# Order of the first modulation groups, shifts of half the channels added as a bias of the input projection, and the first scale group in two halves of 256 columns

## The reference, cut to what matters

```python
mods_x = jnp.split(silu_c @ w_mod[l] + b_mod[l], N_MOD, axis=-1)    # six vectors of 2048
mods_c = jnp.split(silu_cc @ w_mod[l] + b_mod[l], N_MOD, axis=-1)
nc = modulated_norm(h_c, attn_norm[l], mods_c[0], mods_c[1])        # rmsnorm(h) * (1 + scale) + shift
pc = nc @ w_in[l][:, Q_END:KR_END]                                  # 256 + 64 columns
nx = modulated_norm(h_x, attn_norm[l], sa_x, sca_x)
q_a, kv_a, k_rope, g_b, g_c, hh = jnp.split(nx @ w_in[l], [...], axis=-1)   # 512, 256, 64, 3 x 1024 columns
```

## Time and profile before

| | us |
|---|---|
| median of three runs | 1111.26 (1111.02 to 1112.99) |
| span of the profiled execution | 1107.5 |
| between the two | 3.8 |
| PE busy | 1011.4 (91%) |
| VectorE busy | 549.5 (50%) |
| ScalarE busy | 221.2 (20%) |
| GpSimd busy | 20.3 (2%) |
| DMA, mean over the span | 343 GB/s, 380.3 MB |

### The profile page before, as it was taken

One profiled execution on the slowest core, in us unless ns is written; L12 is line 12 of the kernel. 1 busy time (PEld: TensorE's weight loads), 2 busy tenths in 40 slices (PEclk: granted clock), 3 DMA queues, 4 the chain that ended last, 5 costly groups with the idle time before them and its releaser, 6 DMA issues.

```text
span 1107.5 us, 15664 instructions
## 1 busy us (share of the span) xinstructions
PE 1011.4 (91%) x6004; PEld 566.6 (51%) x6005; DVE 549.5 (50%) x1082; ACT 221.2 (20%) x442; POOL 20.3 (2%) x28
## 2 busy tenths in 40 slices
PE   3889999999999889999998999998899898998985
PEld 2534578888885345444485645433334333344421
DVE  3000186854824694985582234545246344545524
ACT  5211110000002363010341213222113112213212
POOL 0000000000002001000000000000000000000002
PEclk9899999999999999999999999999999998999998
DMA  9999979999854747999739999999999999999994
GB/s 358 389 389 389 377 232 359 372 345 328 284 181 169 256 144 262 387 387 335 230 130 367 371 405 403 406 408 407 409 409 406 408 407 408 409 407 408 409 406 180
DMA packets 158359, 380.30 MB, mean 343 GB/s; under 512 B 10498, under 2 KB 44112, under 8 KB 157136
## 3 DMA queue, kind: packets, MB, share of 16 engines
q1 hardware_dynamic: 158288, 379.35, 91.3%
HBM read 377.22 MB, written 2.10 MB: 342 GB/s over the span
## 4 chain that ended last, share of the span: by engine, by line
PE 64%; DMA 13%; SPq 12%; DVE 6%; issue 2%; ACT 2%; POOL 0%; ACTq 0%; DVEq 0%; POOLq 0%
PE ps L654 64%; DMA ring<-in_w_exp_down 7%; SPq L537 4%; SPq L532 4%; DVE part L1590 3%; DMA ring<-in_w_exp_up 2%; DMA ring<-in_w_in 1%; DMA ring<-in_w_mod 1%; DMA qnT<-in_w_mod 1%; SPq L397 1%; DVE tiny L1736 1%; SPq L417 1%; DVE xres L2021 1%; SPq L394 1%; SPq L395 0%
## 5 line engine op out<-in xcount | busy, mean ns | idle before, releaser
L654 PE MATMUL ps<-nreg,ring 128*128 128x256 f32 (+2 forms) x1312 | 306.9, 398 | 6.7 <-DVE ring L1741 4.1
L654 PEld LDWEIGHTS ps<-nreg,ring 128*128 128x128 f32 (+1 forms) x1312 | 243.8, 190 | 63.1 <-issue 30.8
L1590 DVE SCALAR_TENSOR_TENSOR part<-ring,csT,part 128x512 f32<-128x512 f32 x232 | 174.7, 753 | 8.6
L654 PE MATMUL ps<-ring,nreg 128*32 128x512 f32 (+1 forms) x1344 | 174.2, 602 | 3.6 <-DMA ring<-in_w_exp_up 3.2
L654 PE MATMUL ps<-ring,conv 128*32 128x512 f32 (+2 forms) x688 | 104.5, 663 | 23.0 <-DMA ring<-in_w_exp_down 22.1
L654 PE MATMUL ps<-ring 128*128 128x512 f32 x256 | 110.7, 592 | 0.0
L654 PEld LDWEIGHTS ps<-ring,nreg 128*32 128x32 f32 (+1 forms) x1344 | 49.1, 115 | 111.7 <-issue 111.6
L2021 DVE TENSOR_TENSOR xres<-xres,ps 128x512 f32<-128x512 f32 x96 | 61.6, 683 | 48.9 <-PE ps L654 48.9
L654 PEld LDWEIGHTS ps<-ring 128*128 128x128 f32 x256 | 48.6, 190 | 60.4 <-issue 60.0
L654 PEld LDWEIGHTS ps<-ring,conv 128*32 128x32 f32 (+2 forms) x688 | 30.2, 125 | 88.4 <-issue 83.9
L654 PE MATMUL ps<-pick,qnT 128*128 128x128 bf16 x384 | 67.8, 221 | 2.8 <-DMA ring<-in_w_exp_up 2.8
(11 more groups left out here) (265 smaller groups left out, 883.9 us busy)
## 6 DMA issues: line engine op xcount, KB each, us to landing
ring<-in_w_mod SPq DMA_DIRECT2D x78, 1024.0 KB, 10.9
ring<-in_w_exp_gate SPq DMA_DIRECT2D x128, 512.0 KB, 13.6
ring<-in_w_exp_up SPq DMA_DIRECT2D x128, 512.0 KB, 15.1
ring<-in_w_exp_down SPq DMA_DIRECT2D x128, 512.0 KB, 14.4
ring<-in_w_in SPq DMA_DIRECT2D x12, 2048.0 KB, 13.4
ring<-in_w_out SPq DMA_DIRECT2D x8, 2048.0 KB, 11.6
ring<-in_w_mod SPq DMA_DIRECT2D x3, 2048.0 KB, 19.7
ring<-in_w_in SPq DMA_DIRECT2D x3, 1664.0 KB, 15.7
```

Of the source, the lines that this page charges most:

```text
L654: return nc.tensor.matmul(o, l, r, start=start, stop=stop)
L1590: ins = V.scalar_tensor_tensor(out=out_, in0=w_, scalar=scale, in1=acc_, op0=ALU.mult, op1=ALU.add)
```

## The change

It does six things.

1. The groups come in the order scale 0, scale 1, scale 2, shift 2, scale 3, shift 3, shift 0, shift 1 (`MOD_ORDER`). Sets 0 and 1 are projected with scaled, unshifted tokens; sets 2 and 3 as before.
2. For sets 0 and 1 (`LATE = 2`) the product of the shift with the input weights is made by itself (`shift_products`), turned into columns (`bias_columns`) and added as a bias where ScalarE and VectorE read the projection's results. The latent tokens of these sets get their shift added by VectorE behind their last query use, for the convolution (`nT_shift`).
3. The first scale group is loaded as two halves of 256 columns (each half over all 16 row blocks, rows of 1 KB), with the first input-weight slice between and behind them, and worked in halves (`half_rows`, `half_cols`, `first_scale`).
4. Each group's row transposes move behind a projection block. The latent transposes start before the small columns.
5. The first convolution iteration is written out by itself. Its first block runs in two parts around the shift products; the statistics and the key rotation (`in_squares`) run in it, behind the first block of the second slice. GpSimd adds the squares of the channel blocks, so PE sums one product each. On VectorE the bias and the gains stand between the accumulations of groups 8 and 9.
6. The second convolution slice waits for `shift_full` 2 where it waited for `q_full` 1. Some semaphores are merged, with the counts that belong to them.

The core of the diff, SyncE first, then PE:

```diff
-        MOD_ORDER = [g for s in range(4) for g in (s, s + 4)]
+        MOD_ORDER = [4, 5, 6, 2, 7, 3, 0, 1]
+        LATE = 2
...
-            for s in range(2):
-                sp.dma_start(k_of(s, 8), mod_block(MOD_ORDER[0], 8 * s, 8)).then_inc(w_full[s], 16)
+            for h in range(2):
+                at = MOD_ORDER[0] * 512 + 256 * h
+                sp.dma_start(k_of(h, KC), wm[:, :, at:at + 256]).then_inc(w_full[h], 16)
+                for ks in (slice(2, 4),) if h else (slice(0, 1), slice(1, 2)):
+                    load_in(0, ks)
...
-            for s in range(1, 4):
-                for n in (2 * s, 2 * s + 1):
-                    load_early(n)
-                if s == 1:
-                    sp.wait_ge(mod_rows, 1)
-                load_in(s)
+            sp.wait_ge(mod_rows, 1)
+            load_in(1, slice(0, 4))
+            load_early(2)
+            load_in(2, slice(0, 4))
+            load_early(3)
+            load_early(4)
+            load_in(3, slice(0, 4))
+            for n in (5, 6, 7):
+                load_early(n)
...
             load_group(8, 12, mslot, freed_by_pe)
-            sp.wait_ge(q_full, 1)
+            sp.wait_ge(shift_full, 2)
             load_conv(0, 1, CONV0 + 2 * CW)
...
+            query_set(0, (0, 2), (0, 1))
+            pe.wait_ge(xT_ctx, KC // 2)
+            query_set(0, (1, 3), (0, 1))
+            pe.wait_ge(first_dve, 2)
+            half_rows(1)
+            rotary_set(0, (0, 1))
+            kv_set(0, 0, (0, 1))
+            half_cols(1)
+            kv_set(0, 1, (0, 1))
+            query_set(0, range(4), (2, 3))
+            pe.wait_ge(modT_done, 1)
+            second_rows()
+            rotary_set(0, (2, 3))
+            kv_set(0, 0, (2, 3))
+            mod_cols_of(1, 1, 7)
+            kv_set(0, 1, (2, 3))
+            for s in range(1, SETS):
+                query_set(s, range(4))
+                step_group(2 * s)
+                kv_set(s, 0)
+                mod_cols_of(2 * s, 0, 7)
+                step_group(2 * s + 1)
                 rotary_set(s)
+                mod_cols_of(2 * s + 1, 1, 7)
                 kv_set(s, 1)
...
+            def shift_products():
+                pe.wait_ge(shift_ready, LATE)
+                pe.wait_ge(q_sq, 4)
+                for bank, at, end in ((2, 0, QL), (3, QL, WI)):
+                    for k in range(4 * LATE):
+                        ins = mm(ps[32 * (k % 4):32 * (k % 4) + 32, bank, 0:end - at], shift_cols[:, k, :],
+                                 wiq[k // 4][:, k % 4, at:end], k < 4, k >= 4 * LATE - 4)
+                    ins.then_inc(shift_full, 1)
...
+            def in_squares():
+                pe.wait_ge(sq_added, 2)
+                mm(ps[:, 7, 0:T], ones, q_squ[:, 0:T], True, True).then_inc(stat_full, 1)
+                pe.wait_ge(kr_sum, 1)
+                mm(ps[:, 6, :], cst[:, C_DUP:C_DUP + P], krs[:, :], True, True)
+                mm(ps[:, 7, T:2 * T], cst[:, C_ROTK:C_ROTK + P], krs[:, 0:T], True, True).then_inc(kr_mm, 1)
+                pe.wait_ge(kv_out, 1)
+                pe.wait_ge(sq_added, 3)
+                mm(ps[:, 4, :], ones, squ[:, 1024:1536], True, True).then_inc(stat_full, 1)
...
-            with pe.Fori(0, 4) as i:
+            pe.wait_ge(w_full[0], 16 * 3)
+            pe.wait_ge(q_sq, 2)
+            first_conv(range(4 * LATE, KC))
+            shift_products()
+            first_conv(range(4 * LATE))
+            bias_columns()
+            conv_blocks(0, 0, BANKS_C, (1,))
+            conv_blocks(0, 1, BANKS_H, (0,))
+            in_squares()
+            conv_blocks(0, 1, BANKS_H, (1,))
+            pe.wait_ge(kv_out, 2)
+            mod_sum_cols(8, 0)
+            pe.wait_ge(gc_out, 2)
+            pe.wait_ge(mean_wide, 2)
+            conv_blocks(0, 2, BANKS_B)
+            mod_sum_cols(9, 1)
+            with pe.Fori(1, 4) as i:
```

And VectorE, from the last shifts to the loop:

```diff
+            accumulate(8, 0, by_feature=True)
+            ve.wait_ge(shift_full, 3)
+            V.tensor_copy(tiny[:, 16:28], ps[:, 7, 384:396])
+            V.tensor_copy(tiny[0:64, 28:30], ps[0:64, 7, 396:398]).then_inc(shift_ready, 1)
...
             kv_gain(0)
-            ve.wait_ge(stat_q, 1)
+            kv_gain(1)
+            ve.wait_ge(stat_full, 1)
+            ve.wait_ge(kr_mm, 1)
+            ve.wait_ge(q_out, 4)
             mean_square_wide(rowq, ps[:, 7, 0:T], QL)
...
+            accumulate(9, 1, by_feature=True)
+            conv_rows(0)
+            conv_products(0)
+            with ve.Fori(1, 4) as i:
+                accumulate(2 * i + 8, 0, by_feature=True)
+                accumulate(2 * i + 9, 1, by_feature=True)
+                conv_rows(i)
+                conv_products(i)
```

More of the change, by code:

```diff
@@ L1267, in _ @@
                     .then_inc(xT_ctx, 1)
[L1268 to L1269 removed]
             sc.wait_ge(xT_ctx, KC // 2)
[L1271 to L1278 removed]
+            for s, ks in ((0, (0, 1)), (0, (2, 3)), (1, range(4, 8)), (2, range(8, 12)), (3, range(12, 16))):
+                if s == 0 and ks[0] == 2:
+                    sc.wait_ge(mod_rows, 1)
+                    copy(part[:, 0, 256:512], ps[:, 7, 256:512]).then_inc(part_full, 1)
+                for n in ((), (1,), (2, 3), (4, 5))[s]:
+                    rows_out(n, 7, n % 2, n == 1)
+                sc.wait_ge(amul_ready, s + 1 + (ks[0] > 0))
+                for k in ks:
+                    if s < LATE:
+                        ins = nc.scalar.activation(nT[:, k, T:2 * T], nT[:, k, T:2 * T], ACT.Identity, scale=amul[:, k, 1:2])
+                    else:
+                        ins = nc.scalar.activation(nT[:, k, T:2 * T], nT[:, k, T:2 * T], ACT.Identity, bias=modT[:, k, 1:2],
+                                                   scale=amul[:, k, 1:2])
+                    ins.then_inc(nT_ctx, 1)
@@ L1281, in _ @@
             for m in range(4):
                 sc.wait_ge(q_full, m + 1)
-                nc.scalar.activation(squ[:, T * m:T * m + T], ps[:, m, 0:T], ACT.Square).then_inc(q_sq, 1)
+                copy(q_raw[:, m, :], ps[:, m, 0:T]).then_inc(q_sq, 1)
+            for n in (6, 7):
+                rows_out(n, 7, n % 2, False)
+            for n in range(2):
+                sc.wait_ge(shift_full, n + 1)
+                at, end, bank = ((0, QL, 2), (QL, WI, 3))[n]
+                copy(shift_rows[:, at:end], ps[:, bank, 0:end - at]).then_inc(shift_out, 1)
@@ L1284, in _ @@
+            sc.wait_ge(shift_ready, LATE + 1)
+            for m in range(4):
+                sc.wait_ge(q_sq, m + 1)
+                nc.scalar.activation(q_squ[:, T * m:T * m + T], q_raw[:, m, :], ACT.Square, bias=in_bias[:, m, 0:1])\
+                    .then_inc(q_sq, 1)
             sc.wait_ge(kr_full, 1)
-            copy(krs[:, :], ps[:, 6, :]).then_inc(kr_sum, 1)
+            for v in range(2):
+                ins = nc.scalar.activation(krs[:, T * v:T * v + T], ps[:, 6, T * v:T * v + T], ACT.Identity,
+                                           bias=in_bias[:, 6, v:v + 1])
@@ L1612, in _ @@
+            latent_out(range(4))
+            small_out()
+            latent_out((4, 5))
             ve.wait_ge(squares, 4)
-            rsqrt(tiny[:, 10:12], stat[:, 2:4], D)
+            V.tensor_scalar(tiny[:, 10:12], stat[:, 2:4], 1.0 / D, EPS, ALU.mult, ALU.add).then_inc(mean_sq, 1)
+            roots[0] += 1
+            latent_out((6, 7))
+            ve.wait_ge(root, roots[0])
             V.tensor_scalar(ctxs[:, 0, :], ctxs[:, 0, :], tiny[:, 10:11], None, ALU.mult).then_inc(ctxs_ready, 1)
-            cols_out(0, MOD_ORDER[0], 7)
@@ new lines, in _, with scale_of @@
+            first_scale(0)
+            first_scale(1)
+            def scale_of(n):
+                cols_out(n, MOD_ORDER[n], 7)
+                ve.wait_ge(modT_done, n + 1)
+                at = 4 * MOD_ORDER[n]
+                link(V.tensor_tensor(modT[:, at:at + 4, :], modT[:, at:at + 4, :],
+                                     bT[:, at:at + 4].unsqueeze(2).to_broadcast([P, 4, 2]), ALU.add))
+                return V.scalar_tensor_tensor(out=amul[:, at - 16:at - 12, :], in0=modT[:, at:at + 4, :], scalar=1.0,
+                                              in1=vecT[:, V_AN + at - 16:V_AN + at - 12].unsqueeze(2).to_broadcast([P, 4, 2]),
+                                              op0=ALU.add, op1=ALU.mult)
@@ new lines, in shift_of @@
+            def shift_of(n, out_):
+                cols_out(n, MOD_ORDER[n], 7)
+                ve.wait_ge(modT_done, n + 1)
+                at = 4 * MOD_ORDER[n]
+                return V.tensor_tensor(out_, modT[:, at:at + 4, :], bT[:, at:at + 4].unsqueeze(2).to_broadcast([P, 4, 2]), ALU.add)
+            for s in range(1, SETS):
+                n = (0, 1, 2, 4)[s]
+                if s < LATE:
+                    scale_of(n).then_inc(amul_ready, 1)
+                else:
+                    link(scale_of(n))
+                    shift_of(n + 1, modT[:, 4 * s:4 * s + 4, :]).then_inc(amul_ready, 1)
+                ve.wait_ge(amul_ready, s + 2)
```

(15 more changed lines are left out.)

310 lines of the change are left out of this document (153 added, 157 removed).

## The result

| | before | changed |
|---|---|---|
| median | 1110.84 us (1107.23 to 1112.99, 20 runs) | 1111.97 us (1108.31 to 1114.62, 20 runs) |
| ratio, 95% interval | | 1.0018 (1.0010 to 1.0026) |
| span of the profiled execution | 1107.5 | 1109.8 |
| second iteration starts | 189.53 | 189.42 |
| projection behind the convolution starts | 319.28 | 321.07 |

By the ratio the changed kernel is slower by 2.0 us (the two medians lie 1.1 apart), where a gain of 0.6 was forecast. The time itself lies inside the range; the sign is wrong. One execution among those of the experiments, 1200 us in `e3_fill`, fell into a slow state of the chip and is left out of its ratio.

What follows compares the result with a forecast made beforehand. The head was taken as bound by transfers, the convolution stage by PE. With VectorE's chain limiting the gain, 1.8 us won less 1.2 lost to the clock is 0.6: 1111.3 - 0.6 = 1110.7 us, range 1105.0 to 1114.5.

Steps and rivals of the forecast that it cites:

- The landing of group 3: In the head, this modulation group lands at about 74 us; PE waits about 8 us for it, in pieces.
- that of group 5: In the head, this group lands at 100.8 us; PE waits for it and ends its last rows at 101.8.
- the unbroken stretch of PE behind it: From 101.8 us, behind group 5, PE works without a stop; later transfers are hidden.
- the head's win: Up to the convolution stage: it effectively begins at 139.1 us against 146.5 before, 7.4 us earlier.
- VectorE's chain: In the first convolution iteration, VectorE's ordered work behind the key rotation (158.8 us) ends with sum 8's copy at 186.6.
- the wait that it makes: Before group 9's sum, PE arrives at 181.3 us and waits 5.3; the second iteration starts at 187.7, 1.8 us earlier.
- a fall costs up to 1.8 us: Half clock behind PE's wait for sum 8's copy costs between 0 and 1.8 us; 1.2 was taken.
- covered by the 1.9 us for which PE waits at group 5: In the head, a clock fall behind the wait for group 3 is hidden by PE's 1.9 us wait at group 5.
- (1): Rival in the first convolution iteration: VectorE's chain doesn't bind, the head's 7.4 us and 1 us more stay, 1103; chance 0.08.
- (2): Rival in the head: transfers let PE through at group 5, the whole chain 1.9 us earlier, 1107.5 to 1108.9; chance 0.17.
- (3): Rival near 150 us: the second convolution slice lands late; at 15.7 us it costs 3.8, giving 1114.5; chance 0.15.
- (4): Rival after 101.8 us: the clock also falls in PE's unbroken stretch, 1.8 us more, 1112.5; chance 0.10.

Runs made afterwards that it cites:

- e3_fill: Changed kernel plus eleven matmuls of 256 columns, results unread, where PE waits for VectorE's copy of sum 8: 1110.14 us, 1.0001 of the kernel before.
- e1: Changed kernel with PE summing each odd group behind the first convolution block of the next iteration: 1106.46 us, 0.9972 of the kernel before.
- e5: Changed kernel with the first scale group loaded in rows of 2 KB, ahead of the input weights, still worked in halves: 1109.48 us, 1.0005 of the kernel before.
- e2: Changed kernel with the statistics products and key rotation one convolution block earlier on PE: 1104.18 us, 0.9948 of the kernel before.
- e3b: Same edit to the changed kernel as e3_fill, run again for a profile: 1108.76 us for one execution.
- e4: Changed kernel with six linked VectorE instructions, 2.73 us in all, ahead of the accumulation of group 9: 1114.48 us, 1.0040 of the kernel before.
- e6: Changed kernel with rotary products and half a key/value block put between the quarters of groups 3 and 5: 1110.07 us, 1.0012 of the kernel before.
- e8: Changed kernel with statistics products one block earlier and the first scale group in rows of 2 KB: 1103.63 us, 0.9951 of the kernel before.

## Why the prediction was wrong

**What held.** The landing of group 3 (74 forecast, 74.5), that of group 5 (100.8 forecast, 100.24 in `e1`, partly because the halves cost 0.9 by `e5` and not 1.2), the unbroken stretch of PE behind it, the head's win (7.4 forecast; 7.3 in `e2`, which has both the win and no wait), the shift products and bias columns (4.65 forecast, 4.46), VectorE's chain (27.8 forecast, 27.4) and the wait that it makes (5.3 forecast, 4.9). The waits for group 3 come to 5.4 us where about 8 were forecast; its landing sets the end either way. So the mechanism of the forecast is the right one: what the head wins, PE loses again waiting for the copy of sum 8.

**The step that failed** is one sentence under "The clock": "a fall costs up to 1.8 us", from which I took 1.2. It failed twice.

- Behind the 4.9 us wait a fall costs 2.7 us by `e3b` against the changed kernel; against the terms of the sum it is 2.6, since I had given 1.0 for the four narrow products: they took 1.70, and the second iteration 1.90 more. 1.4 over what I took, 0.8 over the bound. The one row that I priced it from was a fall of 3.4 us (12.2 less 10.3 is 1.9, not 1.8, which changes nothing here); this one lasts 6.8.
- Behind the wait for group 3 I called it "covered by the 1.9 us for which PE waits at group 5". It costs 2.9 us, and 1.6 come through (`e1`, which has the same waits and no fall, against the changed kernel), so the cover is 1.3. That moved VectorE's chain, and with it everything. This half rests on one trace without the fall against two with it.

The account, at the end of the second iteration: 0.6 less in the forecast, 1.8 more in the trace (233.74 against 231.95). The statistics late, 1.5; VectorE's chain shorter, -0.4; the clock behind the wait, 1.4: 2.5, for a difference of 2.4.

**The rule of the Trainium skill** that I weighed, "TensorE: Matmul & The Clock Gate", section "HAM oscillation", was the right one here: the wait of 4.9 us or more for sum 8 had the clock at half behind it in every trace here that has it (both of the changed kernel, `e4`, `e5`, `e6`). Taking the value between the two rows was a choice against it, and the trace of before had the second fall from 24 to 32 us as well, which speaks for the rule too. The place of the fall behind short waits isn't settled by it: `e1` had the same four waits as the changed kernel and kept its clock.

**The rivals.** (1), VectorE's chain not binding, is refuted by the wait and by `e4`; what it would have given, 1103, is near what `e2` measured with the chain moved (1104.18). (2), PE passing group 5 early, occurred in its outward sign alone: group 5 wasn't waited for, but because PE was late (101.84 for the last quarter, against 100.24 in `e1`). (3), the second convolution slice, didn't occur: its transfer is issued at 139.58 and PE shows no wait for it at 150. (4), a fall in the unbroken stretch, didn't occur there; of the forecast's own kind, at a wait, there were two.

**What stays open.** Why the clock falls behind the waits for group 3 in the other traces that have them (both of the changed kernel, `e2`, `e3b`, `e4`) and not in `e1`'s is not shown. Nor is what makes a fall 3.4 or 6.8 us long: behind single waits of 2.46 and 4.04 us it was 3.4 (the kernel before, `e5`), behind 4.26 and 4.90 us 6.8 (`e8`, the changed kernel). Where it fell decided its price: in `e2`, `e3b` and `e4` it fell one wait earlier (the row at 71.74 above, eight row matmuls in 1.94 us, has it), part of it lay under the wait for the last quarter, and the statistics started at 157.1 to 157.5 (in `e2` after adding the 6.9 us of the block by which they were moved), against 158.3 to 158.5 for the two executions of the changed kernel. And behind the head, from the first expert transfer to the first output transfer, the traces differ by up to 4.7 us (528.0 in `e6` to 532.7 in `e2`; 529.4 before, 529.5 changed) with no relation to the head. That scatter is as large as what is argued about here, so the points of the account rest on the traces up to 321 us, and only the sign and the rough size on the medians.

## What to carry to other kernels

Before moving the work of one engine earlier, follow the explicit waits to the first point where it meets the other engine's in-order chain, and ask when that chain's first input is made: here one line that put four products a block ahead turned a loss of 2 us into a gain of 6. A wait that replaces another is not of equal worth if the engine behind it is TensorE: price it as the wait plus the half-clock stretch behind it. The length of the wait alone doesn't give the length of that stretch (4.04 and 4.26 us of waiting, 3.4 and 6.8 us of half clock, in `e5` and `e8`), so read all falls in the trace, and let the bound be twice the dearest one seen: 3.6 here, which would have covered the 2.7 and 2.9. That factor is an estimate from this case and was not tried elsewhere.

## What the runs showed of the hardware

- The half clock behind a wait of 4.9 us lasted 6.8 us and cost 2.7, that behind four waits of 0.6 to 1.7 us lasted 6.8 and cost 2.9; the two falls of the kernel before, behind waits of 2.17 and 2.46 us, lasted 3.4 each.
- Waits of nearly the same length had falls of different length behind them: 4.04 us in `e5` 3.4 (0.89 and 0.69 from 24 to 32 us), 4.26 us in `e8` 6.8 (0.81, 0.50 and 0.84 from 24 to 36 us); the work behind took 1.2 us longer in the second.
- Keeping PE busy with 22 matmul instructions whose result nobody reads removed the fall whole, and the kernel became faster with more work (`e3b`).
- The same four waits had a fall behind them in the changed kernel, twice, and none in `e1`.
- Transfers with rows of 1 KB moved 376 GB/s from 20 to 40 us, with rows of 2 KB 391.
